# Key blocks laid from the first key on, the remaining 16 keys as one corner product per bank, and a reordered head, w_out entry and tail, in a hybrid attention and convolution block

## The reference, cut to what matters

```python
h = concat([meta_tokens (16), x (1024)])            # 1040 tokens of 1024 channels
hn = rmsnorm(h) * mix_norm_g
q, k, v, ca, cg = split(hn @ w_in)                  # 8 heads of 64; 512 conv channels
# stick-breaking attention, per head, s < t only, z = q.k/8:
#   A[t,s] = sigmoid(z_ts) * prod_{s<j<t} (1 - sigmoid(z_tj));   attn = A @ v
conv = silu(layernorm(depthwise_conv31(ca * sigmoid(cg)) + b))
h = h + concat([attn, conv]) @ w_out
h = h + (silu(rmsnorm(h) @ w_gate) * (rmsnorm(h) @ w_up)) @ w_down   # 2816 hidden columns
return rmsnorm(h)[16:]                               # the meta tokens are dropped
```

## Time and profile before

| | |
|---|---|
| median of three runs | 1216.48 us |
| profiled execution, whole | 1215.46 us |
| its span, first to last instruction | 1213.6 us |
| granted TensorE clock, mean | 0.995 |
| head, until PE starts V's second block | 0 to 23 us |
| projections and pairs 0 to 3 | 56 to 424 us |
| w_out stage | 417 to 522 us |
| FFN and tail | 522 to 1213.6 us |

### The profile page before, as it was taken

One profiled execution on the slowest core, in us unless ns is written; L12 is line 12 of the kernel. 1 busy time (PEld: TensorE's weight loads), 2 busy tenths in 40 slices (PEclk: granted clock), 3 DMA queues, 4 the chain that ended last, 5 costly groups with the idle time before them and its releaser, 6 DMA issues.

```text
span 1213.6 us, 15537 instructions
## 1 busy us (share of the span) xinstructions
PE 1173.6 (97%) x6108; PEld 1003.4 (83%) x6108; DVE 679.7 (56%) x737; ACT 421.1 (35%) x785; POOL 480.2 (40%) x365
## 2 busy tenths in 40 slices
PE   6999999999999999989999999999999999999996
PEld 5899899899898878867888888888888888888875
DVE  5349995986958846695343434343434343434346
ACT  5311451541645644454222222222222222222223
POOL 4112301301300003256737373737373737373721
PEclk9999999999999999999999999999999999999998
DMA  7203202203107011112121212121212121212113
GB/s 273 79 9 98 70 19 71 70 2 81 25 12 251 10 52 35 36 52 70 35 70 36 70 35 70 35 70 36 70 35 70 35 70 35 70 35 70 35 53 139
DMA packets 65334, 75.50 MB, mean 62 GB/s; under 512 B 6064, under 2 KB 54828, under 8 KB 65262
## 3 DMA queue, kind: packets, MB, share of 16 engines
q1 hardware_dynamic: 64078, 72.38, 19.1%
q10 hardware_dynamic: 1184, 2.13, 0.5%
HBM read 63.92 MB, written 6.32 MB: 58 GB/s over the span
## 4 chain that ended last, share of the span: by engine, by line
PE 70%; POOL 12%; issue 8%; DVE 6%; ACT 2%; DMA 1%; SPq 0%; POOLq 0%; ACTq 0%; DVEq 0%
PE ps L1662 19%; PE ps L1641 17%; PE ps L1467 12%; PE ps L1530 6%; PE ps L1590 5%; POOL wa_lo L588 4%; PE ps L1428 4%; PE ps L1515 3%; PE ps L1497 3%; POOL wb_lo L588 2%; DVE acc L1108 2%; POOL wa_f L609 1%; POOL wa_f L603 1%; POOL wa_f L606 1%; DMA out<-ost 1%
## 5 line engine op out<-in xcount | busy, mean ns | idle before, releaser
L1348 DVE TENSOR_TENSOR mix<-ps,mix 128x512 f32<-128x512 f32 x176 | 121.3, 691 | 137.6 <-PE ps L1662 137.6
L1108 DVE SCALAR_TENSOR_TENSOR acc<-u_pad,par,acc 128x1024 f32<-128x1024 f32 x116 | 146.7, 1303 | 0.3
L540 POOL TENSOR_TENSOR wp_lo<-raw,wp_hi 128x1024 fp32r<-128x1024 f32 x16 | 61.9, 3868 | 202.3 <-ACT wp_hi L687 202.3
L1662 PE MATMUL ps<-wd_hi,act_hi 128*128 128x512 f32 x352 | 137.0, 389 | 1.5 <-DVE act_lo L1337 1.5
L1662 PE MATMUL ps<-wd_hi,act_lo 128*128 128x512 f32 x352 | 136.9, 389 | 0.0
L1662 PE MATMUL ps<-wd_lo,act_hi 128*128 128x512 f32 x352 | 136.9, 389 | 0.0
L588 POOL TENSOR_TENSOR wa_lo<-wa_f,wa_hi 128x512 fp32r<-128x512 f32 x58 | 79.4, 1371 | 133.3 <-ACT wa_hi L909 129.4
L1467 PE MATMUL ps<-hn_hi,wp_hi 128*128 128x348 f32 (+2 forms) x352 | 118.4, 336 | 0.0
L1467 PE MATMUL ps<-hn_lo,wp_hi 128*128 128x348 f32 (+2 forms) x352 | 117.7, 334 | 0.0
L1467 PE MATMUL ps<-hn_hi,wp_lo 128*128 128x348 f32 (+2 forms) x352 | 117.6, 334 | 0.0
L1641 PE MATMUL ps<-t_hi,wa_hi 128*128 128x512 f32 x232 | 91.8, 396 | 4.2 <-POOL wa_lo L588 3.9
(11 more groups left out here) (161 smaller groups left out, 2585.3 us busy)
## 6 DMA issues: line engine op xcount, KB each, us to landing
raw<-in_w_gate SPq DMA_DIRECT2D x11, 1024.0 KB, 5.3
raw<-in_w_up SPq DMA_DIRECT2D x11, 1024.0 KB, 5.3
wd_f<-in_w_down SPq DMA_DIRECT2D x11, 1024.0 KB, 4.9
raw<-in_w_in SPq DMA_DIRECT2D x16, 512.0 KB, 3.9
xin<-in_x SPq DMA_DIRECT2D x8, 512.0 KB, 10.9
wo_raw<-in_w_out SPq DMA_DIRECT2D x4, 1024.0 KB, 8.1
mix<-in_x SPq DMA_DIRECT2D x8, 512.0 KB, 3.5
out<-ost SPq DMA_DIRECT2D x8, 512.0 KB, 2.6
```

The lines of the kernel that those rows point to most:

```text
L540: pool.tensor_tensor(dst, raw[:, slot, :], hi.bitcast(F32), ALU.subtract).then_inc(wlo_done, 1)
L1108: dve.scalar_tensor_tensor(out=acc[:, j % 2, :], in0=u, scalar=w, in1=acc[:, j % 2, :], op0=ALU.mult, op1=ALU.add).then_inc(conv_step, 1)
L1348: dve.tensor_tensor(hrow, ps[:, TB + n % 4, :], hrow, ALU.add).then_inc(d_added, 1)
L1662: last = pe.matmul(ps[:, TB + n % 4, :], a[s][:, t, i * P:(i + 1) * P], w_[m][:, t, dh * BANK:(dh + 1) * BANK], start=(t == 0 and s == m = ...
```

## The change

Key blocks start at the first key. A tile i has i + 1 full blocks, and 16 keys remain behind them (those of its last queries). For the tile's first 112 queries all 16 are masked, so that their running product is 1 there and these queries need only the value of the blocks' last key as bias (v_edge). For its last 16 queries they are a 16 x 16 corner of gq. For the four tiles of a PSUM bank and both heads ACT copies these 16 columns side by side into g_corner (8 x 16 columns), PE transposes it once, DVE multiplies it with a 0/1 pattern that keeps each (tile, head) on its own 16 rows (`spread`), and one product per bank adds it for 4 x 16 query columns (`attend_corner`). The bias differs between the first 112 queries and the last 16 (v_last), so the eviction is made in two pieces per tile. The eviction of a pair moves behind the next pair's first groups; in the last pair the two banks are evicted around the entry to w_out, whose parts are reordered. In the head the norm weights are loaded as one row and spread by PE, the first x tile comes before the meta tokens, and V's first block is split. In the tail the squares go to a buffer of their own, ost has three buffers, and the last tile is squared, scaled and stored in halves.

```diff
-    KB = T // P + 1
+    KB = T // P
-        nb = i + 2
+        nb = i + 1
         return [range(a, min(a + 4, nb)) for a in range(0, nb, 4)]
...
+        CORNER = (Z + 1, TB)
+        def ms_of(i, part):
+            if (i, part) == (1, 0):
+                return [qst[:, s_, 0:4 * P].rearrange("p (k t) -> p k t", k=4) for s_ in range(2)]
+            return ms_hi[:, part, :, :], ms_lo[:, part, :, :]
...
# SP, head and pair_loads
-            load_x(1)
-            load_x(0)
-            sp.dma_start(g1b[:, :], mix_norm_g[0].partition_broadcast(P)).then_inc(g1_loaded, 16)
+            sp.dma_start(g1row[:, :], mix_norm_g[0:1, :]).then_inc(g1_loaded, 16)
+            load_x(0)
+            load_x(1)
+            load_wv(0)
+            load_x(2)
+            for j in range(1, 4):
+                load_wv(j)
...
+                sp.dma_start(v_edge[:, p, :], v_dram[0:KB * P, bass.ds(P * p, P)].rearrange(
+                    "(i t) c -> t c i", t=P)[P - 1], allow_slow_non_contiguous=True).then_inc(last_loaded, 16)
...
+                if p == 0:
+                    sp.wait_ge(v_zeroed, 4)
+                    for h in range(2):
+                        for j in range(4):
+                            rows = slice(DH * h + META * j, DH * h + META * (j + 1))
+                            src = v_dram[P:P + KB * P, :].rearrange("(b j t) c -> j t b c", b=2, j=4)
+                            sp.dma_start(vc[rows, :, :], src[j, 0:META]).then_inc(vc_loaded, 16)
+                            for b in range(2):
+                                r = P * (4 * b + j + 1) - 1
+                                src = v_dram[r:r + META, :].rearrange("t (p h c) -> t p h c", p=PAIRS, h=2)
+                                sp.dma_start(vc_of[rows, :, b, DH * h:DH * h + DH], src[:, :, h]).then_inc(vc_loaded, 16)
...
# ACT
+            def evac_attention(p, g):
+                act.wait_ge(corner_used, 2 * p + g + 1)
+                for i in range(4 * g, 4 * g + 4):
+                    if i == 1 and p == PAIRS - 1:
+                        mix_hi(0, 0)
+                    for cols, last_key in ((slice(0, IN_CORNER), v_edge), (slice(IN_CORNER, P), v_last)):
+                        last = act.activation(mix[:, i, p, cols], ps[:, PV + g, (i % 4) * P + cols.start:(i % 4) * P + cols.stop],
+                                              ACT.Identity, bias=last_key[:, p, i:i + 1])
+                last.then_inc(pv_evac, 1)
...
                     sigmoid_gate(p + 1, range(2 if p else 0, 3))
+                    for g in range(2 if p else 0):
+                        evac_attention(p - 1, g)
...
                 split_hi("q", 0, p)
+                if not more:
+                    for g in range(2):
+                        evac_attention(p - 1, g)
                 split_hi("k", 2, p)
...
# ACT, at the end of copy_t(n)
+                    act.activation(g_corner[:, i // 4, at:at + META], gq[:, n % BUFS, P * (i + 1):P * (i + 1) + META],
+                                   ACT.Copy).then_inc(corner_copied, 1)
...
# ACT, pair
-                    if n == FIRST_HALF + 2:
-                        evac_attention(0, FIRST_HALF)
-                        if not more:
-                            mix_hi(0, 0)
+                    if n == NU - 1 and not more:
+                        evac_attention(p, 0)
+                        act.wait_ge(pv_evac, past(NG * PAIRS - 1))
+                        mix_hi(1, 0)
...
-                    mix_hi(1, 0)
-                evac_attention(1, NU - 1)
+                    evac_attention(p, 1)
...
# DVE, head
             for t in range(TILES + 1):
                 lo_x(t)
                 if t == 1:
-                    for j in range(3):
+                    norm_x(2)
+                    for j in range(4):
                         wv_low(j)
-                if t + 2 <= TILES:
+                if t and t + 2 <= TILES:
                     norm_x(t + 2)
-                if t == 1:
-                    wv_low(3)
...
# DVE, pair
+            def spread(p, b):
+                dve.wait_ge(corner_ready, 2 * p + b + 1)
+                corner = ps[:, CORNER[b], IN_CORNER:P].unsqueeze(1).to_broadcast([P, 4, META])
+                dve.tensor_tensor(corner_w[:, b, :, :], corner, own_tile[:, :, :], ALU.mult).then_inc(corner_spread, 1)
...
                     some_taps(p, now, len(now) - 8)
+                    if p:
+                        spread(p - 1, 1)
...
-                    if not more and n == NU - 2:
-                        mix_lo(0, 0)
                 assert more or not now
+                spread(p, 0)
                 if p + 2 == PAIRS:
                     for g in range(2):
                         split_lo("k", g, p + 1)
+                    spread(p, 1)
+                if not more:
+                    mix_lo(0, 0)
+                    spread(p, 1)
...
# DVE, w_out stage
             for i in range(TILES):
                 if i >= 1:
                     residual(i - 1)
+                if i + 1 < TILES:
+                    ln_stats(i + 1)
                 mix_lo(i, 1)
                 if i >= 2:
                     lo_h(i - 2)
                 if i + 1 < TILES:
-                    ln_stats(i + 1)
                     ln_normalise(i + 1)
...
# PE
+            for b in range(2):
+                pe.matmul(ps[:, PJ + b, :], ones_1[:, :], g1row[:, b * BANK:(b + 1) * BANK],
+                          start=True, stop=True).then_inc(g1_spread, 1)
...
+            def transpose_corner(p, b):
+                if b == 0:
+                    pe.wait_ge(z_free, past(NZ * (p + 1)))
+                pe.wait_ge(corner_copied, NU * p + (NU if b else FIRST_HALF + 1))
+                pe.transpose(ps[:, CORNER[b], 0:P], g_corner[:, b, :], ident[:, :]).then_inc(corner_ready, 1)
+            def attend_corner(p, b):
+                if p == b == 0:
+                    pe.wait_ge(vc_stepped, 4)
+                pe.wait_ge(corner_spread, 2 * p + b + 1)
+                out_of = ps[:, PV + b, :].rearrange("p (i t) -> p i t", i=4)[:, :, IN_CORNER:P]
+                pe.matmul(out_of, vc_of[:, p, b, :], corner_w[:, b, :, :], start=False, stop=True,
+                          skip_group_check=True).then_inc(corner_used, 1)
...
-                groups(todo[2:-1])
+                groups(todo[2:3])
+                for b in range(2 if p else 0):
+                    attend_corner(p - 1, b)
+                groups(todo[3:-1])
...
+                    if n == NU - 3:
+                        transpose_corner(p, 0)
                     if n:
                         attend(n - 1)
-                    if n < NU and n != 1:
-                        transpose_w(n, range(2, nb))
+                    if n == NU - 2 and p == PAIRS - 1:
+                        attend_corner(p, 0)
+                transpose_corner(p, 1)
...
             def first_tile():
                 ln_forward(0)
-                w_out_part(0, 0)
-                ln_backward(0)
...
             pair(PAIRS - 1, {NU: first_tile})
-            pe.wait_ge(pv_evac, past(NG * PAIRS))
+            w_out_part(0, 0, lambda: attend_corner(PAIRS - 1, 1))
+            ln_backward(0)
```

More of the change, by code:

```diff
@@ L183, in hybrid_block @@
         sumsq = keep("sumsq", [P, 3 * (TILES + 1)], F32)
+        own = keep("own", [P, 2, 4, META], F32)
+        own_tile = keep("own_tile", [P, 4, META], F32)
+        sumsq_1 = keep("sumsq_1", [P, 2], F32)
         var = keep("var", [P, 3 * (TILES + 1)], F32)
@@ L732, in _ @@
             square_x(1)
+            wv_high(0)
             square_x(2)
@@ L1089, in split_lo @@
                     last = dve.tensor_tensor(dst, src, high.bitcast(F32), ALU.subtract)
+                    if kind == "q" and h == 0:
+                        last.then_inc(q_low, 1)
                 last.then_inc(pj_free_dve, 1)
@@ L1257, in _ @@
             ln_normalise(0)
-            for k in range(4, 7):
+            mix_lo(1, 0)
+            for k in range(4, 8):
                 w_out_lo(k)
-            mix_lo(1, 0)
-            w_out_lo(7)
             for i in range(TILES):
@@ L1421, in project_v @@
                 if b == 0:
-                    order = [(k, 0, 0) for k in range(KD)] + [(k, 1, 0) for k in range(KD)] + [(k, 0, 1) for k in range(KD)]
+                    order = ([(k, s, 0) for ks in (range(KH), range(KH, KD)) for s in range(2) for k in ks]
+                             + [(k, 0, 1) for k in range(KD)])
                 else:
                     order = [(k, s, m) for k in range(KD) for s, m in PASSES]
-                for n, (k, s, m) in enumerate(order):
+                for n, (k, s, m) in list(enumerate(order))[part]:
+                    if b == 0 and (k, s) == (0, 1):
+                        pe.wait_ge(xlo_ready, 2)
                     if b == 0 and s == 0 and k % 2 == 0:
@@ L1524, in attend @@
                         pe.wait_ge(v_zeroed, 4)
-                    ends = [n_ for n_, u in enumerate(UNITS) if u[1] // 4 == i // 4]
```

(1 more changed line is left out.)

237 lines of the change are left out of this document (154 added, 83 removed).

## The result

The changed kernel takes 1206.98 us (median of 6 runs, 1205.63 to 1208.28), the kernel before, on the same chip, 1216.38: a ratio of 0.9924, 95% interval 0.9911 to 0.9936, some 9.4 us faster. The forecast was 1197.0 with a range of 1190.5 to 1204.5, and the result lies outside it: the sign was right, the size was not, and half of the expected gain is missing. The profiled execution took 1206.98 with a span of 1205.0.

The account below looks back on a forecast made before the run. PE was taken as the bound, with DVE pacing pair 3. Gains of 0.9 + 12.1 + 1.5 + 1.3 + 3.7 = 19.5 gave 1215.5 - 19.5 + 1.0 = 1197.0 us, range 1190.5 to 1204.5.

Parts of the forecast that it names:

- Head: Term for the start: less DMA ahead of the x tile lets V's second block start earlier, 0.9 us gained.
- w_out stage: Term: statistics taken before lo_h on DVE end ln_backward's wait of 0.33, four times, 1.3 us gained.
- tail: Term for the end: separate square buffer, three output buffers, last tile in halves, 3.7 us gained.
- What PE saves: Step for the attention pairs: dropped key blocks save PE 5.3 us per pair, less corner transposes and products at 0.22 each.
- PE's full saving: Rival: scans come earlier too, 4.9 us per pair and 2.5 in the head, 1193 us; chance 0.09.
- Pairs 0 to 2: Term for the first three attention pairs: 3.9, 3.9 and 4.3 us, together 12.1 gained, with ACT's added work hidden.
- ACT or DVE holds the pairs: Rival: ACT's 32 added instructions push scans back, half of the pairs' 12.1 us stays, 1203 us; chance 0.14.
- Pair 3: Term for the last pair and entry to w_out: 2.0 us gained less 0.5 for DVE's late start, 1.5.
- the clock: Rival: new PE waits lower its granted clock; one fall under 2 us, four 7, 1204 us; chance 0.03.
- FFN: Term: the stage has the same list on every engine and moves as a whole, nothing gained.
- 24 small DMAs: Weighed rule: SP's 24 corner loads in pair 0, at 0.6 us each, never make DVE wait; counted as nothing.
- the stall at 2.07 per DMA: Rival: pair 0's corner loads delay PE, by 8.5 us at 2.07 us per DMA, 1205.5; chance 0.03.

Follow-up runs that it names:

- b1: The kernel before with v_dram 128 rows taller, rows that nothing reads or writes: 1216.44 us, ratio 0.9998 to the kernel before.
- a4: The changed kernel with POOL taking only 8 columns of each projection weight's low part from the fifth weight on, the rest left out: 1195.67 us.
- a1: The changed kernel with the sixteen evictions moved behind the high part of the k weights on ACT in pairs 1 and 2: 1201.45 us.
- a5: The changed kernel with POOL's making of the 0/1 patterns own and own_tile moved to the start, where POOL is idle: 1203.93 us.
- c1: The changed kernel with evictions behind k's high part, pair 3's first corner spread behind unit 14's scan, and own and own_tile made early: 1197.41 us.
- b5: The kernel before with ACT taking k's high part of pairs 1 and 2 one projection group later: 1219.39 us, ratio 1.0038.
- c2: c1 with DVE instead of POOL taking the low part of the q weights of pairs 0 to 2, behind the taps' sum: 1197.39 us.
- a3: The changed kernel with the old tail: two output buffers, squares written into them, the last tile whole: 1209.7 us.
- d1: The changed kernel with 18 unused semaphore increments on PE behind the two products that spread the norm's row: ratio 0.9906 to the kernel before.
- c3: c1 with 48 unused semaphore increments at the start of PE's program: ratio 0.9877 to the kernel before.
- c4: c1 with ACT taking k's high part of pairs 1 and 2 one projection group later: 1200.71 us, ratio 0.9884.
- c5: c1 with 18 unused semaphore increments on PE behind the two products that spread the norm's row: 1196.65 us.

## Why the prediction was wrong, and where it was right

**Head (0.9; measured 1.17), w_out stage (1.3; 1.40), tail (3.7; 3.76): right**, by the steps given. V's second block starts at 21.67, from 22.84; DVE's list, by which I had it at 21.9, ends at 21.55. The head is the least certain of the three: in the other profiles of kernels with the change and no added code its gain runs from 0.4 to 1.6, and b1, with the head of before, took 1.0 longer than before. In the w_out stage ln_backward waits for nothing. Of the tail, the old one put back gives 3.1 to 3.7.

**What PE saves: right, even low.** Corner products took 0.2 each, as assumed. In a4 the period falls by 4.87, the 4.9 that the rival "PE's full saving" had; I had taken 3.9 (4.3 less the corner products) because the scans would stay where they were. They follow PE, once nothing else holds DVE.

**Pairs 0 to 2 (12.1; measured 5.7): the step that failed** is the sentence on ACT: 16 corner copies and 8 more evictions, "hidden by the 9 of 20 in which ACT is idle" and by its waits for PE. I weighed the evictions against copies that PE waits for. What stands behind them on ACT is the high part of k, behind that POOL's low part, and this ran into DVE's taps. Its price, 2.1 in each of pairs 1 and 2 (a1: 4.24), is not in ACT's time at all; in pair 0 the select on POOL did the same (a5: 1.9). POOL's subtractions and selects were in none of my steps. The rival that came nearest, "ACT or DVE holds the pairs", had 1203, still 4 from the result, and another mechanism: scans pushed back by the added ACT instructions themselves. With these collisions moved away c1 has 11.86 of the 12.1.

**Pair 3 (1.5; measured -0.39).** The lateness of the corner was seen and rightly priced: 1.4 behind the scan's end (0.6 later than before, since the scan comes earlier); the trace has 1.38. Where the clock didn't fall (a1, a5) the term is 1.2, near the 1.5. The step that failed is that the sum left out the fall of the clock, 1.6. I had it as a rival ("the clock", 0.03), with new waits at just these places and a price under 2 us: right in size, too small in chance. With the corner moved ahead and no fall (c1) the term is 2.57, better than forecast.

**FFN (0; measured -2.99): the second step that failed**, "has the same list on every engine and moves as a whole". The lists are the same, but packets of PE's code run beside the weights' on the DMA queues, and with other code ahead they fall elsewhere: 2.5 of the 2.99 come at three loads that such a packet meets, less the one that it no longer meets.

**24 small DMAs: right at nothing.** SP issued most of them 0.6 us apart, from 137.4 to 152.9 us, and DVE never waited for them. Issue to landing, in the page's last part:

```profile
vc<-v_dram SPq DMA_DIRECT2D x8, 64.0 KB, 2.3
vc_of<-v_dram SPq DMA_DIRECT2D x16, 16.0 KB, 2.0
```

So each takes 2.0 to 2.3 us from issue to landing, near the 2.0 us that the Trainium skill gives ("DMA: Bandwidth & Descriptors", Anatomy of one DMA; the section is on DMAs that GpSimd issues, and these are SP's), but beside the next and not after it.

The profile's tests that I had named did point at it: of the signs for wrong, "PE waiting in mid-pair" came true, for u_pad and scans, and so did "a granted clock below 1 in the attention" (0.91 from 400 to 420 us). The pair period was 84.31 and not 82.0, and DVE's idle stretch 7.83 and not 10.5. Slips in the prediction's sums change nothing: what PE saves before unit 15 is 4.5 and not 4.6, PE's list in pair 3 ends at 418.5 and not 418.7, and the stall at 2.07 per DMA is 8.6 and not 8.5.

## What to carry to other kernels

When work is put ahead of something on one engine, follow what stands behind it through every engine to where it lands in time, and ask whom it meets there: here some 3 us of evictions on ACT cost nothing on ACT and 2.1 us per pair on DVE, by way of POOL. The slack that counts is that of the nearest hand-over, not that at the end of the stage. Take POOL's subtractions and selects to stretches in which DVE is idle, even setup work of 0.3 us.

## What the runs showed of the hardware that I had not expected

- A POOL instruction of 0.34 us took 8.26 beside an unbroken row of two-input DVE taps (changed kernel), and 0.34 where DVE was idle (a5).
- A subtraction of 2.4 us on POOL cost a two-input DVE instruction 2.1 us (changed kernel, b5), and the same work on DVE is 1.22 (c2).
- With a 16 KB packet of instructions 0.6 to 3.2 us behind its issue, a weight load of 1 MB was in use up to 1.5 us later (36 loads, mean 0.9), though the packet is a 64th of its bytes; an unchanged stage of 656 us so lost some 2.5 when the code ahead of it changed.
- TensorE's granted clock fell in pair 0 in some kernels (a1, a3, d1) and in pair 3 in others (changed, a3, d1), though their instructions there are nearly the same; a fall cost 0.4 to 1.6 us. c1, c3, c4 and c5 had none before the end.
